# One two-block network on one core: the overflow test moved ahead of the last expert step, five warm-up calls, weight splits between the normed tiles, residual scaling on GpSimd moved

## What is computed

```python
def first_block(x, ...):
    x = x + hybrid_mixer(rms_norm(x, g_mix), ...)          # two kinds of attention, gates
    x = x + hier_moe(rms_norm(x, g_moe), ...)              # 32 experts, 2 for each token
    return rms_norm(x, g_final)

def hybrid_layer(x, c, ...):                               # the second block
    shift, scale, gate = split(silu(c) @ w_ada + b_ada, 3)
    h = rmsnorm(x, norm_g) * (1 + scale) + shift
    q, k, v, g_attn, cb, cc, cx, g_conv, m_attn, m_conv = split(h @ w_in)   # 10 x 1024 columns
    ...                                                    # attention, short convolution, merge
    return x + gate * (merged @ w_out)

def second_block(x, ...):
    return rmsnorm(hybrid_layer(x, ...), final_g)
```

## Time and profile before

| | |
|---|---|
| median of 3 runs | 1073.35 us (1071.11 to 1076.58) |
| the profiled execution's own time | 1078.87 us |
| its span in the trace | 1077.1 us |
| PE busy | 1009.5 us, 94% |
| DVE, ACT, POOL busy | 394.1, 368.6, 133.9 us |
| HBM traffic | 286 GB/s mean over the span |

### The profile page before, as it was taken

One profiled execution on the slowest core, in us unless ns is written; L12 is line 12 of the kernel. 1 busy time (PEld: TensorE's weight loads), 2 busy tenths in 40 slices (PEclk: granted clock), 3 DMA queues, 4 the chain that ended last, 5 costly groups with the idle time before them and its releaser, 6 DMA issues.

```text
span 1077.1 us, 14861 instructions
## 1 busy us (share of the span) xinstructions
PE 1009.5 (94%) x6329; PEld 707.1 (66%) x6329; DVE 394.1 (37%) x757; ACT 368.6 (34%) x606; POOL 133.9 (12%) x83
## 2 busy tenths in 40 slices
PE   7999998998999999998989898986999999999996
PEld 6887887976444444433334343335999999999994
DVE  4454446645121212121211111025434443783474
ACT  4546654632111111111111111015345554554442
POOL 1111111211000000000000000003121111242122
PEclk9999999999999999998999999898999999999998
DMA  8975567574899999999999999994445535544400
GB/s 291 352 251 201 200 238 292 195 269 198 341 420 419 419 420 419 420 418 419 421 419 419 420 420 421 418 397 153 164 157 206 184 132 193 194 162 165 168 1 39
DMA packets 83003, 307.92 MB, mean 286 GB/s; under 512 B 6607, under 2 KB 11112, under 8 KB 58352
## 3 DMA queue, kind: packets, MB, share of 16 engines
q1 hardware_dynamic: 79144, 302.16, 71.9%
q10 hardware_dynamic: 3784, 4.73, 1.4%
HBM read 305.81 MB, written 2.63 MB: 286 GB/s over the span
## 4 chain that ended last, share of the span: by engine, by line
PE 71%; DMA 11%; DVE 8%; SPq 4%; ACT 3%; issue 2%; POOL 1%; POOLq 0%; ACTq 0%; DVEq 0%
PE bank L756 69%; DMA arena<-in_w 5%; DMA ring<-in_w 5%; SPq L808 4%; DVE arena L1222 2%; DVE arena L1219 2%; DVE arena L1225 1%; DVE wR L1219 1%; DMA ring<-in_w_in 1%; PE bank L1168 1%; ACT wR L1781 1%; ACT arena L1947 1%; PE bank L940 1%; POOL wR L2111 0%; PE bank L934 0%
## 5 line engine op out<-in xcount | busy, mean ns | idle before, releaser
L756 PE MATMUL bank<-hTR,wR 128*128 128x256 f32 x2520 | 316.4, 286 | 6.4 <-DVE wR L1219 3.6
L756 PEld LDWEIGHTS bank<-hTR,wR 128*128 128x128 f32 x2520 | 307.8, 193 | 11.4 <-issue 10.1
L756 PE MATMUL bank<-ring,arena 128*64 128x512 f32 (+1 forms) x1056 | 232.0, 609 | 7.9 <-DMA ring<-in_w 7.8
L1781 ACT ACTIVATE wR<-ring 128x1024 fp32r<-128x1024 f32 x161 | 168.1, 1053 | 108.5 <-PE bank L756 105.7
L1219 DVE TENSOR_TENSOR wR<-ring,wR 128x1024 fp32r<-128x1024 f32 x121 | 151.1, 1255 | 136.9 <-ACT wR L1781 136.6
L756 PE MATMUL bank<-arena 128*64 128x512 f32 (+7 forms) x778 | 167.5, 540 | 7.4 <-DMA arena<-in_w 6.5
L756 PEld LDWEIGHTS bank<-ring,arena 128*64 128x64 f32 (+1 forms) x1056 | 70.0, 137 | 142.6 <-issue 131.7
L1219 DVE TENSOR_TENSOR arena<-arena,bank 128x256 f32<-128x256 f32 (+1 forms) x36 | 16.0, 450 | 364.1 <-ACT arena L1947 358.5
L1926 ACT ACTIVATE arena<-bank 64x512 f32<-64x512 f32 x64 | 37.9, 592 | 308.1 <-PE bank L756 307.7
L2111 POOL TENSOR_TENSOR wR<-ring,wR 128x1024 fp32r<-128x1024 f32 x40 | 97.3, 2433 | 354.2 <-ACT wR L1781 354.2
L756 PEld LDWEIGHTS bank<-arena 128*64 128x64 f32 (+4 forms) x778 | 65.1, 151 | 94.1 <-issue 82.2
(11 more groups left out here) (204 smaller groups left out, 844.9 us busy)
## 6 DMA issues: line engine op xcount, KB each, us to landing
ring<-in_w SPq DMA_DIRECT2D x120, 1024.0 KB, 25.1
arena<-in_w SPq DMA_DIRECT2D x72, 1024.0 KB, 25.6
ring<-in_w_in SPq DMA_DIRECT2D x30, 2048.0 KB, 8.7
ring<-in_w_ada SPq DMA_DIRECT2D x6, 2048.0 KB, 8.1
ring<-in_w_o SPq DMA_DIRECT2D x2, 2048.0 KB, 8.5
ring<-in_w_o_attn SPq DMA_DIRECT2D x2, 2048.0 KB, 7.9
ring<-in_w_o_conv SPq DMA_DIRECT2D x2, 2048.0 KB, 8.2
ring<-in_w_out SPq DMA_DIRECT2D x2, 2048.0 KB, 9.1
```

Source lines behind the costliest of these rows:

```text
L756: return pe.e.matmul(o, l, r, start=start, stop=stop)
L1781: eng.activation(h, w, ACT.Copy).then_inc(s_high, 1)
```

## The change

Four edits, all around the turn from the first block to the second.

1. `experts` on DVE and ACT no longer does its own tail, but returns it as a function (`last_low`, `finish`). Both engines load the flag and branch ahead of the tail. The tail then stands twice in the program: at the start of the overflow rounds, and in an `Else` block, which these inputs take. PE, POOL and SP test where they did.
2. `warm(pe, banks[7], 36)` becomes `warm(pe, banks[7], 5)`.
3. Pieces 0, 1 and 2: ACT makes the high parts (`early_splits`) ahead of `second_norm`. DVE makes the low part of piece 0 ahead of `second_norm`, and those of pieces 1 and 2 behind the casts of the first and the second normed tile. Before, all three stood between `second_norm` and the first `turn3`.
4. POOL's `residual(n)` moves from behind `second_norm` to the projections, tile 0 behind the step `("evict", "p0", 1)`, tile 1 behind `("evict", "p2", 1)`. ACT waits for both ahead of the evictions of p10 and p11, which write where `XS2` lay.

Smaller things in it: ACT's first squares go to a scratch area of their own, and `s_sums` is raised once by each square rather than by two at the end, so that DVE's first two small ops on a tile can run before the second square is there.

```diff
--- before.py
+++ after.py
@@ -661,11 +661,12 @@
 
         PR = Turn([0, 1, 6])
         O2 = Order(n_pieces1, len(pieces), Loads(n_moe, len(chunks)))
-        for _ in range(3):
-            O2.more()
         for j2 in range(4):
+            if j2 < 3:
+                O2.more()
             PB.use(("hT3", j2), PR.next())
             O2.add("turn3", j2)
+        early_splits = [st for st in O2.steps if st[0] == "split"]
         O2.add("bias", 0)
         for nm in ("p0", "p1", "p2", "p3"):
             project(O2, nm, "h3")
@@ -876,7 +877,7 @@
                 for r in range(1, 4):
                     experts_pe(pe, eng, r, POB, dict(zip(MOE_SEMS, [sem("o" + n) for n in MOE_SEMS])))
             pe.known = known
-            warm(pe, banks[7], 36)
+            warm(pe, banks[7], 5)
             for step in O2.steps:
                 second_steps_pe(pe, eng, *step)
 
@@ -1560,7 +1561,7 @@
                     last.then_inc(x.free, 1)
                     if e and e % 2 == 0:
                         low(e // 2 - 1)
-                low(NE // 2 - 1)
+                return lambda: low(NE // 2 - 1)
 
             def spread(i, r, P, S):
 
@@ -1592,11 +1593,12 @@
                     tt(XS2[:, n, :], XN[:, n, :], gfin, ALU.mult).then_inc(s_xg[n], 1)
                 for n in range(NT):
                     s1, s2, v1, w1, r1, r2 = (tw[:, 2 * m + n:2 * m + n + 1] for m in range(6))
-                    v.wait_ge(s_sums[n], 2)
+                    v.wait_ge(s_sums[n], 1)
                     ts(v1, s1, 1.0 / D, EPS, ALU.mult, ALU.add).then_inc(s_var[n], 1)
                     v.wait_ge(s_var[n], 1)
                     v.step(ts(w1, v1, EPS, None, ALU.mult))
                     v.settle()
+                    v.wait_ge(s_sums[n], 2)
                     stt(w1, s2, 1.0 / D, w1, ALU.mult, ALU.add).then_inc(s_w1[n], 1)
                     if n == 1:
                         v.wait_ge(s_rs[1], 3)
@@ -1740,22 +1742,27 @@
             for step in O1.steps:
                 first_steps(*step)
             route()
-            experts(0, PB, dict(zip(MOE_SEMS, [sem(n) for n in MOE_SEMS])))
+            last_low = experts(0, PB, dict(zip(MOE_SEMS, [sem(n) for n in MOE_SEMS])))
             v.wait_ge(s_flag, 1)
+            known = dict(v.known)
             with eng.If(eng.value_load(flag[0:1, 0:1]) > SLOTS):
-                known = dict(v.known)
+                last_low()
                 v.wait_ge(s_scat, NE // 2)
                 for n in range(NT):
                     add_experts(n, s_ofold)
                 for r in range(1, 4):
                     if r > 1:
                         v.wait_ge(s_oscat, 16 * (r - 1))
-                    experts(r, POB, dict(zip(MOE_SEMS, [sem("o" + n) for n in MOE_SEMS])))
+                    experts(r, POB, dict(zip(MOE_SEMS, [sem("o" + n) for n in MOE_SEMS])))()
                 v.wait_ge(s_oscat, 3 * NE // 2)
                 emptied(v, POB.of["spread", 3, 3])
+            v.known = dict(known)
+            with eng.Else():
+                last_low()
             v.known = known
+            second_steps(*O2.steps[0])
             second_norm()
-            for step in O2.steps:
+            for step in O2.steps[1:]:
                 second_steps(*step)
             final()
 
@@ -1945,17 +1952,20 @@
                     if e > 1:
                         filled(s, P.of["hT", r, e - 2])
                     eng.activation(Hb[e % 2], banks[u.bank][:, 0:256], ACT.Silu).then_inc(S["silu"], 1)
-                down(NE - 1)
-                high(NE // 2 - 1)
+
+                def finish():
+                    down(NE - 1)
+                    high(NE // 2 - 1)
+
+                return finish
 
             def second_norm():
                 tw = sm(0, 12)
                 for n in range(NT):
                     s.wait_ge(s_xsum[n], 1)
-                    s.step(eng.activation(XV[:, n, :], XN[:, n, :], ACT.Square, accum_out=tw[:, n:n + 1]))
+                    eng.activation(area(8 + 4 * n, D), XN[:, n, :], ACT.Square, accum_out=tw[:, n:n + 1]).then_inc(s_sums[n], 1)
                     s.wait_ge(s_xg[n], 1)
-                    s.settle()
-                    eng.activation(XV[:, n, :], XS2[:, n, :], ACT.Square, accum_out=tw[:, 2 + n:3 + n]).then_inc(s_sums[n], 2)
+                    eng.activation(XV[:, n, :], XS2[:, n, :], ACT.Square, accum_out=tw[:, 2 + n:3 + n]).then_inc(s_sums[n], 1)
                 s.wait_ge(s_rs[0], 3)
                 eng.activation(XV[:, 0, :], XS2[:, 0, :], ACT.Copy, scale=tw[:, 10:11]).then_inc(s_norm[0], 1)
 
@@ -2002,6 +2012,8 @@
                     elif i in (10, 11):
                         u = U_[nm, c2]
                         filled(s, u)
+                        for n in range(NT):
+                            s.wait_ge(s_x2done[n], 1)
                         eng.activation(flat2(ccT, 4 * (i - 10) + 2 * c2), banks[u.bank][:, :], ACT.Copy).then_inc(u.free, 1)
                     elif i in (8, 9):
                         u = U_[nm, c2]
@@ -2072,20 +2084,27 @@
             for step in O1.steps:
                 first_steps(*step)
             route()
-            experts(0, PB, dict(zip(MOE_SEMS, [sem(n) for n in MOE_SEMS])))
+            finish = experts(0, PB, dict(zip(MOE_SEMS, [sem(n) for n in MOE_SEMS])))
             s.wait_ge(s_flag, 1)
+            known = dict(s.known)
             with eng.If(eng.value_load(flag[0:1, 0:1]) > SLOTS):
-                known = dict(s.known)
+                finish()
                 s.wait_ge(s_scat, NE // 2)
                 for r in range(1, 4):
                     if r > 1:
                         s.wait_ge(s_oscat, 16 * (r - 1))
-                    experts(r, POB, dict(zip(MOE_SEMS, [sem("o" + n) for n in MOE_SEMS])))
+                    experts(r, POB, dict(zip(MOE_SEMS, [sem("o" + n) for n in MOE_SEMS])))()
                 s.wait_ge(s_oscat, 3 * NE // 2)
+            s.known = dict(known)
+            with eng.Else():
+                finish()
             s.known = known
+            for step in early_splits:
+                second_steps(*step)
             second_norm()
             for step in O2.steps:
-                second_steps(*step)
+                if step not in early_splits:
+                    second_steps(*step)
             s.wait_ge(s_rs[0], 4)
             s.wait_ge(s_fo[0], 1)
             eng.activation(XO[:, 0, :], XO[:, 0, :], ACT.Copy, scale=st3[:, 6:7]).then_inc(s_out[0], 1)
@@ -2127,14 +2146,13 @@
                     p.wait_ge(s_w1[n], 1)
                     rsqrt(tw[:, 10 + n:11 + n], tw[:, 6 + n:7 + n], s_rs[n])
 
-            def residual():
+            def residual(n):
                 tw = sm(0, 12)
-                for n in range(NT):
-                    p.wait_ge(s_var[n], 1)
-                    p.step(eng.tensor_tensor(tw[:, 8 + n:9 + n], tw[:, 4 + n:5 + n], mhalf[:, 0:1], ALU.pow))
-                    p.settle()
-                    p.wait_ge(s_sums[n], 2)
-                    eng.tensor_scalar(XN[:, n, :], XS2[:, n, :], tw[:, 8 + n:9 + n], None, ALU.mult).then_inc(s_x2done[n], 1)
+                p.wait_ge(s_var[n], 1)
+                p.step(eng.tensor_tensor(tw[:, 8 + n:9 + n], tw[:, 4 + n:5 + n], mhalf[:, 0:1], ALU.pow))
+                p.settle()
+                p.wait_ge(s_sums[n], 2)
+                eng.tensor_scalar(XN[:, n, :], XS2[:, n, :], tw[:, 8 + n:9 + n], None, ALU.mult).then_inc(s_x2done[n], 1)
 
             def second_steps(what, *a):
                 if what == "split" and on_pool(a[0]):
@@ -2168,13 +2186,14 @@
                 p.wait_ge(s_oscat, 3 * NE // 2)
             p.known = known
             second_norm()
-            for st in O2.steps[:3]:
-                second_steps(*st)
-            residual()
             p.wait_ge(s_h3, 4)
             eng.memset(U[:, :, 0:2], 0.0).then_inc(s_uz, 1)
-            for st in O2.steps[3:]:
+            for st in O2.steps:
                 second_steps(*st)
+                if st == ("evict", "p0", 1):
+                    residual(0)
+                elif st == ("evict", "p2", 1):
+                    residual(1)
             for n in range(NT):
                 p.wait_ge(s_var[n], 2)
                 rsqrt(st3[:, 6 + n:7 + n], st3[:, 4 + n:5 + n], s_rs[n])
```

## The result

| | before | changed |
|---|---|---|
| median, 20 runs each | 1071.19 us (1068.49 to 1077.18) | 1065.62 us (1062.0 to 1071.38) |
| ratio, 95% interval | | 0.9938 (0.9923 to 0.9953) |
| span of the profiled execution | 1077.1 us | 1067.4 us |

The ratio means 6.6 us of 1071.19, between 5.0 and 8.2; the two medians stand 5.6 us apart. The forecast was 5.9 us.

What follows compares the result with a forecast made beforehand. PE, busy 1009.5 of 1077.1 us, was taken as the bound, with idle time at the turn. 5.5 to 6.2 us, less up to 0.7, plus 0.3, was taken as 5.9: 1073.35 to 1067.4; range 1064.8 to 1071.5.

Steps and rivals of the forecast that it cites:

- The clock: PE around the four normed tiles: 1.2 GHz most of the time until 748.95; tile 0's products end 5.5 to 6.2 us sooner.
- The sum: Whole turn: 5.5 to 6.2 us, less up to 0.7, plus 0.3, giving 4.8 to 6.5; 5.9 us taken.
- a late return: PE's projections: if full clock returns only 4.3 us behind 748.95, the stream loses 0.7 us more.
- the four tiles: DVE's casts and subtractions with two low parts between: fourth normed tile at 750.1 instead of 756.60, 6.5 us sooner.
- the small ops: DVE's small ops ahead of the norms start earlier because the wait is split in two: perhaps 0.3 us more off.
- the calls: PE's warm-up ahead of the transposes: 5 calls, 10 records, take 1.4 to 1.5 us and end before both norms.
- The Else jump: End of the Else block on DVE and ACT: about 0.1 us, with bounds of nothing and 5.5 us.
- rival 2: New jump behind the tail costs a fetch, at most 5.5 us: 1072.9, values between 1068.6 and 1072.9; chance 0.19.
- rival 4: POOL's residual holds DVE's low parts for its whole length: 0.9 us stall for each half, 1069.2; chance 0.04.
- Rival 3: PE's clock stays low through the first tiles for 4 us more: 2 us lost, 1069.4; chance 0.08.
- Rival 5: More than forecast: PE's own test shorter when engines don't fetch at once, and full clock: 1065.5; chance 0.04.
- The warm-up is last, by 3.6 us: Ahead of the transposes: PE's warm-up ends 3.6 us behind the norms; removing it or DVE's test alone gives at most that.

Runs made afterwards that it cites:

- the near test: Changed kernel plus one DVE test between tail and piece 0's low part, jumping over one small memset; turn 25.75 us, ratio 0.9933 against the kernel before.
- low parts last: Changed kernel with DVE's low parts of pieces 1 and 2 behind all four normed tiles; turn 22.82 us, ratio 0.9934 against the kernel before.

## Why the prediction was off, and what was right in it

**The step that failed: the clock.** The forecast has 5.9 us and the trace 7.04. The term that was mis-sized is "The clock": I expected "1.2 GHz there most of the time" up to 748.95. The sum charged 0.3 to 1.0 us for it behind the fourth tile, and up to 0.7 us more for a late return. The trace shows no charge. The clock was at 2.4 GHz from 12.5 us behind the start of the tail and stayed there, and from the fourth tile to the end of the turn it took 5.10 us, against 5.21 before. That is 1.0 of the 1.1 us. The other 0.1 us is DVE's: the four tiles gave 6.93 us and not 6.5 + 0.3. The 0.3 for the small ops came true at the norms (7.86 us from the first addition to `s_norm[1]` instead of 8.2), but it reached nobody, since PE came later. What did reach the end is that a low part costs 1.14 us of DVE's time and not 1.25, and the next cast starts 1.06 us behind a cast where no low part stands between them, not 1.15.

Why the clock stays up is not settled. PE worked without a pause from 735.91 on, because the calls lasted longer than I had said; but without any calls it rose as well, and with the near test, whose PE program is the same, it fell again and the turn was 25.75. That is 5.8 us less than before: had the changed kernel's trace met this fall, the forecast would have looked exact. So part of a hit would have been luck, and so is part of this miss.

**Two errors that cancelled.** The first step of transposes ends 11.68 us behind the start of the tail (739.27; 19.19 before): 7.5 us sooner, as forecast. The sum behind it was wrong twice. I priced the calls at 1.4 to 1.5 us from the 7 records in a window of 1 us, but a window counts also the records that only reach into it: four windows of 1 us from 738.66 on count 24, one of 4 us counts 18. Ten records took 2.50 us and ended at 738.41, 0.26 us behind `s_norm[1]` at 738.15, so that the calls were last and not the norm. And the 0.45 us of the transposes, which I took as their time at half clock, had been measured at full clock; at 1.2 GHz they took 0.87. Against both stood the norm, 10.56 us behind the tail and not 11.2. That the end fits to 0.1 us is luck.

**The starting point.** 1073.35 was the median of three runs, 2.2 us above that of twenty. From 1071.19 the same forecast gives 1065.2, and the runs, with 5.0 to 8.2 us, can't tell 5.9 from 7.0. It took both the mis-sized clock and the high start to bring 1064.6 below the range.

**Right.** Both tests hide in the idle time, with the 5.77 and 7.30 us unchanged. The Else jump costs nothing, so rival 2 is out. DVE starts its additions 4.3 us sooner behind the tail (6.96 to 2.70; 4.0 forecast), since they wait for six of the scatter's eight matmuls and not for its end. The casts fell to 0.42 us. POOL's residual in the projections holds nobody up: DVE's low part of piece 4 beside it takes 1.23 us in the changed kernel and 1.90 at most in the others, far from the 3 us that are spare, and rival 4 is out. Rival 3 is out. Rival 5 had the full clock, with 0.04, but for a shorter test on PE, and PE's next call did not move.

**Wrong in the reading of before.** "The warm-up is last, by 3.6 us" compared PE with the norms only. The instruction that uses the transposes first is a cast on DVE, and DVE stood at low parts until 0.65 us before it. With the calls alone cut, 0.9 us came out and not 3.3. Of the summed result this changes nothing, because the change also moved the low parts; but as a statement on what bounds the stretch it was wrong.

**What each edit is worth.** Tests and calls together 4.9 us (0.9 and 1.7 alone). The residual 2.6 in its one trace, of which 1.45 are casts and the rest the clock. The splits -0.3 (-0.8 when the tiles are done): I had booked them as 2.5 us of cost between the tiles, rightly, but did not see that in their old place, once the calls are few, they fill a wait. With all edits, the low parts are best behind the fourth tile (1.7 us more). Whole runs bear out the sum, that tests and calls together are faster than before (0.9956, at most 0.9981), and that the calls matter once the rest is changed (0.9938 with 5 and 1.0017 with 36, intervals apart). The other steps stand in one trace each.

## What to carry to other kernels

When two engines arrive late at the same place, look also at what the consumer of their work is doing until then: here a third queue, DVE's low parts, was 0.65 us behind the first; cutting one alone gave 0.9 or 1.7 us, cutting both 4.9. A runtime test that jumps far cost its engine about 5 us here, and the load and the comparison were not what took the time; it is free if it stands in a wait of that length, at the price of having the rest of the loop body twice in the program. Padding work such as warm-up calls covers other work; when it goes, look at what it covered. And a count of records in a short window is no rate.

## What the runs showed of the hardware

- A test with a far jump costs 4.4 to 5.6 us on PE and DVE, and PE's next call stands at 8.3 to 8.4 us behind the start of DVE's tail in every trace with calls, whether the scatter ahead of the test took 2.1 or 3.0 us; a test that jumps over one instruction costs under 1.4 us, and the jump at the end of the Else block none that can be seen. Packets on an instruction queue pass beside the far tests and none beside the near one. By the rule of the Trainium skill, "Runtime: NRT & Kernel Launch", section "Instruction fetch mechanics" (a taken branch stalls only if its target is not among the pages held), this is what should come out; the trace agrees, and adds the size. The far tests of these traces ran beside weight loads, 300 to 390 GB/s on average over each; what one costs beside an idle DMA no run shows.
- When DVE and POOL's scaling (2.85 us alone) run together, time is lost. Of DVE it was a cast (1.02 to 1.27 us instead of 0.42) or a subtraction (1.41 instead of 0.69, with casts of 0.42 just before and behind it). POOL's scaling took 2.85 us beside such casts, 3.54 beside that subtraction, and 3.8 to 4.0 where it and a low part of DVE's started within 0.12 us of each other. Where the low part started 0.29 us behind POOL (low parts last), DVE took 1.90 us for it instead of 1.23, and POOL 2.86. DVE never waits for the whole of the other, as "SBUF — State Buffer" of the Trainium skill, section "Who interferes with whom", would have it: a cast that starts 0.13 us behind POOL's 2.85 us loses 0.85.
- TensorE's clock rose behind some 3.1 to 5.3 us of unbroken work at 1.2 GHz in most traces, whether the work was warm-up calls or the transposes alone, and behind 2.2 us in the kernel before, at 756.6 (the prediction read 1.9). With PE busy for 2.0 of 5 us it stayed up in three traces of the changed kernel and fell in that of the near test, whose PE program is the same, at a price of 1.2 us.
